# A dilated mixer taken head pair by head pair: values first, attention steps between projections

## The chip, the cores and the metric

The kernel runs on one core of one Trainium2 chip. Time is device microseconds (us) of that core. TensorE multiplies matrices into PSUM, which has eight banks of 512 columns; VectorE and ScalarE work on vectors; GpSimd and SyncE here do little but issue DMA.

## What is computed

A model of two transformer blocks and a second part, on 256 tokens of width 1024. The change lies in the second block's mixer, the dilated one: three groups of 16 heads of 64, each with its own window and dilation, combined by the softmax over all three groups' scores.

```python
DIL_GROUPS = ((128, 1), (512, 4), (2048, 16))
...
proj = (h @ w_in).reshape(B, S, N_DIL_GROUPS, 3, DIL_HEADS, DIL_HEAD_DIM)
for gi, (window, dilation) in enumerate(DIL_GROUPS):
    q = rms_norm(proj[:, :, gi, 0], g_q[gi])
    k = rms_norm(proj[:, :, gi, 1], g_k[gi])
    v = proj[:, :, gi, 2]
    ...
    o, lse = dilated_group(q, k, v, pos, table, window, dilation)
...
wts = jax.nn.softmax(jnp.stack(lses, axis=0), axis=0)
o = jnp.einsum('gbsh,gbshd->bshd', wts.astype(o_all.dtype), o_all)
return o.reshape(B, S, DIL_HEADS * DIL_HEAD_DIM) @ w_o
```

Inside a group, scores are q k / 8 plus a bias looked up by the distance of the positions, with a window mask.

## The kernel before

Five programs are written out by hand, one for each engine, and they meet in semaphores. Each program walks the same list of **units** (`PLAN`): a unit is 128 x 1024 weights, loaded by SyncE into one of four raw buffers, split by ScalarE into a high half (`wh`, line 851) and by VectorE into the rest (`wl`, line 1359), with three split buffers. On ScalarE and VectorE, entering unit u (`unit`, `ahead`) makes the halves of unit u+2, and ScalarE waits there for TensorE to have finished unit u-1. TensorE then runs 24 matmuls a unit: high by high, high by rest, rest by high (lines 346 to 348).

In the mixer the units are, for each of three groups, 16 of queries and keys (`dil_qk`, each 128 outputs of one of six kinds z) and 8 of values (`dil_v`). Two units of one kind fill a bank. Then the head norm: ScalarE squares the bank, TensorE sums the squares over each head (`head_sums`), ScalarE makes mean and root and squares the root, VectorE refines it and scales the bank into `qk` (`head_norm`). Beside the first units runs `bias(0)`: TensorE multiplies comparisons (`step`, made by VectorE) with the bias table, VectorE adds the mask into `B`. Every few units VectorE multiplies a row of modulation weights (`araw`, `tick`), whose DMA GpSimd issues.

After all 72 units come 32 attention steps, 16 heads for the first 128 tokens and 16 for the second, with `bias(1)` alone between them, because `B` holds one table. A step i does the scores of i (`s1`), turns the weights of i-2 (`s2`) and multiplies those of i-3 with the values (`s3`). VectorE adds the bias and finds the maximum, ScalarE takes the exponential, VectorE normalizes, ScalarE copies the turned weights to a buffer of three. Then `residual` runs 8 output units (`dil_w_o`), each giving 128 outputs; after each pair VectorE updates the residual `xT`, and ScalarE squares it for the next norm.

PSUM banks are taken from a queue in order of release (`take`, `give`): TensorE waits for the reader of the bank at its head. What decides the order around the change is the text of these loops.

## Time and profile before

| | us |
|---|---|
| median of 3 runs | 2232.82 (2232.3 to 2234.47) |
| the profiled execution | 2235.26 |
| its span | 2233.2 |
| TensorE busy in the span | 2035.8 |
| VectorE busy | 1459.5 |
| ScalarE busy | 1089.2 |
| issue to landing of a load of `dil_qk` | 3.7 |
| issue to landing of a load of `dil_v` | 4.2 |

All times in the rows are us from the span's start. TensorE's matmuls overlap, so the pitch from one start to the next tells more than a duration. The granted clock is a share of 2.4 GHz. In the stretches the busy times come in the order PE (TensorE), PEld (its weight loads), DVE (VectorE), ACT (ScalarE), POOL (GpSimd), each with its count of instructions. In a timeline a row "x2" is two operations from the first's start to the last's end; brackets give the idle time ahead and what ended it.

### The profile page before, as it was taken

To read this page: it belongs to the slowest core of one execution; us is meant where nothing else is said; L and a number is where in the kernel's file an instruction comes from. 1 tells how busy PE (TensorE), PEld (TensorE's weight loads), DVE (VectorE), ACT (ScalarE), POOL (GpSimd) and SP (SyncE) were. 2 spreads that over 40 slices of the span, in tenths; PEclk is the share of its full clock that TensorE was granted. 3 is DMA by queue.
4 is the path that set the end of the run, shared out by engine and by line. 5 is a ranking of instruction groups with operands and counts; after the bars stand their busy time and mean duration, and the time that the engine had idled before them with its cause. 6 is when DMAs were issued, how large, how long until landed. Compare 5 with 4: busy or idle time off the path is not lost.

```text
span 2233.2 us, 34387 instructions
## 1 busy us (share of the span) xinstructions
PE 2035.8 (91%) x14140; PEld 1873.7 (84%) x14140; DVE 1459.5 (65%) x2577; ACT 1089.2 (49%) x1676; POOL 172.2 (8%) x243
## 2 busy tenths in 40 slices
PE   2768999899999998998978889999999879999998
PEld 2646999789998978998858889999999767888886
DVE  6696885666766556744755444888886696555554
ACT  3544553335664145543654444444444695444444
POOL 3020000000000000000000000000000393000000
PEclk7879999889999699999899999999999999999999
DMA  6534687425554014665413434555555303555553
GB/s 261 195 118 147 209 282 250 157 95 201 205 170 147 10 52 157 189 189 165 175 66 123 146 122 158 171 189 184 185 188 183 112 1 113 189 188 189 188 189 122
DMA packets 97083, 356.20 MB, mean 160 GB/s; under 512 B 10704, under 2 KB 10832, under 8 KB 96544
## 3 DMA queue, kind: packets, MB, share of 16 engines
q1 hardware_dynamic: 83824, 305.04, 40.7%
q0 software_dynamic: 12672, 48.08, 6.9%
q8 instruction: 111, 1.82, 0.3%
q10 hardware_dynamic: 432, 0.90, 0.1%
q14 instruction: 44, 0.36, 0.1%
HBM read 352.93 MB, written 1.05 MB: 159 GB/s over the span
## 4 chain that ended last, share of the span: by engine, by line
PE 79%; DVE 15%; ACT 4%; DMA 1%; issue 1%; SPq 0%; POOL 0%; DVEq 0%; ACTq 0%
PE psum L346 23%; PE psum L347 22%; PE psum L348 22%; PE psum L339 10%; DVE C L1331 2%; PE psum L353 1%; DVE wl L1359 1%; DVE araw L1342 1%; DVE one L1331 1%; ACT work L839 1%; DVE one L1336 1%; DVE work L1339 1%; DMA first<-in_ada_w 1%; DVE first L1342 0%; ACT sqh L839 0%
## 5 line engine op out<-in xcount | busy, mean ns | idle before, releaser
L1359 DVE TENSOR_TENSOR wl<-raw,wh 128x1024 fp32r<-128x1024 f32 (+1 forms) x564 | 686.5, 1222 | 466.2 <-ACT wh L851 465.2
L851 ACT ACTIVATE wh<-raw 128x1024 fp32r<-128x1024 f32 (+1 forms) x564 | 592.7, 1052 | 466.0 <-PE psum L348 466.0
L346 PE MATMUL psum<-peer_hh,wh 128*128 128x256 f32 x1152 | 325.4, 282 | 4.1 <-DVE peer_hl L1331 4.0
L347 PE MATMUL psum<-peer_hl,wh 128*128 128x256 f32 x1152 | 324.5, 282 | 0.0
L348 PE MATMUL psum<-peer_hh,wl 128*128 128x256 f32 x1152 | 324.4, 282 | 0.0
L346 PEld LDWEIGHTS psum<-peer_hh,wh 128*128 128x128 f32 x1152 | 217.8, 189 | 5.4 <-DVE peer_hl L1331 4.4
L347 PEld LDWEIGHTS psum<-peer_hl,wh 128*128 128x128 f32 x1152 | 218.1, 189 | 0.0
L348 PEld LDWEIGHTS psum<-peer_hh,wl 128*128 128x128 f32 x1152 | 218.0, 189 | 0.0
L346 PE MATMUL psum<-wh,csh 128*128 128x512 f32 x512 | 202.3, 395 | 0.0
L347 PE MATMUL psum<-wl,csh 128*128 128x512 f32 x512 | 202.2, 395 | 0.0
L348 PE MATMUL psum<-wh,csl 128*128 128x512 f32 x512 | 202.2, 395 | 0.0
L346 PE MATMUL psum<-mlp_hh,wh 128*128 128x256 f32 x512 | 148.1, 289 | 8.3 <-DVE mlp_hl L1339 8.3
L347 PE MATMUL psum<-mlp_hl,wh 128*128 128x256 f32 x512 | 145.9, 285 | 0.0
L348 PE MATMUL psum<-mlp_hh,wl 128*128 128x256 f32 x512 | 145.8, 285 | 0.0
L347 PE MATMUL psum<-h1l,wh 128*128 128x256 f32 x512 | 144.1, 281 | 0.0
L346 PE MATMUL psum<-h1h,wh 128*128 128x256 f32 x512 | 144.1, 281 | 0.0
L348 PE MATMUL psum<-h1h,wl 128*128 128x256 f32 x512 | 144.1, 281 | 0.0
L346 PE MATMUL psum<-dil_hh,wh 128*128 128x256 f32 x448 | 137.9, 308 | 6.0 <-DVE dil_hl L1339 4.1
L347 PE MATMUL psum<-dil_hl,wh 128*128 128x256 f32 x448 | 130.2, 291 | 0.0
L348 PE MATMUL psum<-dil_hh,wl 128*128 128x256 f32 x448 | 130.2, 291 | 0.0
L346 PEld LDWEIGHTS psum<-wh,csh 128*128 128x128 f32 x512 | 96.0, 187 | 23.5
L348 PEld LDWEIGHTS psum<-wh,csl 128*128 128x128 f32 x512 | 96.0, 187 | 23.5
(412 smaller groups left out, 4603.4 us busy)
## 6 DMA issues: line engine op xcount, KB each, us to landing
raw<-in_mlp_w SPq DMA_DIRECT2D x128, 512.0 KB, 4.1
raw<-in_eu SPq DMA_DIRECT2D x128, 512.0 KB, 3.3
raw<-in_ev SPq DMA_DIRECT2D x128, 512.0 KB, 3.2
araw<-in_ada_w POOLq DMA_DIRECT2D x80, 512.0 KB, 4.2
raw<-in_dil_qk SPq DMA_DIRECT2D x48, 512.0 KB, 3.7
raw<-in_dil_v SPq DMA_DIRECT2D x24, 512.0 KB, 4.2
first<-in_ada_w SPq DMA_DIRECT2D x8, 1024.0 KB, 18.2
raw<-in_w_in SPq DMA_DIRECT2D x16, 512.0 KB, 3.3
```

What stands on the lines that cost most here:

```text
L339: i = e.matmul(o, l, r, start=start, stop=stop, skip_group_check=loose)
L346: e.matmul(o, l[0], r[0], start=start, stop=False, skip_group_check=loose)
L347: e.matmul(o, l[0], r[1], start=False, stop=False, skip_group_check=loose)
L348: i = e.matmul(o, l[1], r[0], start=False, stop=stop, skip_group_check=loose)
L353: t = e.transpose(o, i, ident)
L839: e.activation(o, i, f, **kw).then_inc(S.act, 1)
L851: e.activation(b.wh[v % NSPLIT][:, 0:cols], b.raw[v % NRAW][:, 0:cols], ACT.Copy).then_inc(S.hi, 1)
L1331: return op(e.tensor_tensor(o, x, y, f), mark)
L1336: return op(e.tensor_scalar(o, x, s1, s2, f0, f1), mark)
L1339: return op(e.scalar_tensor_tensor(out=o, in0=x, scalar=s, in1=y, op0=f0, op1=f1), mark)
L1342: return op(e.tensor_tensor_reduce(out=o, in0=x, in1=y, scale=1.0, scalar=init, op0=f0, op1=f1, accum_out=acc), mark)
L1359: e.tensor_tensor(b.wl[v % NSPLIT][:, 0:cols], b.raw[v % NRAW][:, 0:cols], b.wh[v % NSPLIT][:, 0:cols].bitcast(F32), ALU.subtract).then_in ...
```

## The change

The mixer is taken head pair by head pair. `dil_order` writes out one order that all programs follow. First 18 of the 24 value units (heads 0 to 11), with both bias tables beside them; `B` now holds both. Then for each pair c its six query and key units (z = 0 to 5: query and key of three groups, so a bank holds the query and key of one group), the head norms of pair c, and between them the steps of pair c-1. The roots of a pair's three groups are taken together, one pair later, behind unit z=1 of the next pair; their squares and the scales follow behind z=2 and z=3. The last six value units stand behind the last pair, and then the output units, which are now rows of the output matrix: each takes one head pair's output and adds to all 1024 outputs, in four banks that are read at the very end. The turned weights have one buffer in place of three. The modulation products come once in four value units and once in two query and key units.

```diff
+def dil_order():
+
+    values = [("dil_v", 8 * g + x, x // 2) for g in range(3) for x in range(8)]
+    out = [e for e in values if e[2] < 3] + [("biased", 0, 0)]
+    summed = []
+
+    def after_unit():
+        if summed:
+            c, g = summed.pop(0)
+            out.append(("sum", c, g))
+            if g:
+                out.append(("mean", c, g))
+
+    for c in range(8):
+        steps = {4: 4 * c - 4, 5: 4 * c - 3, 0: 4 * c - 6, 1: 4 * c - 5}
+        for z in range(6):
+            out.append(("dil_qk", 8 * z + c, z))
+            after_unit()
+            if z == 3:
+                out.append(("mean", c, 0))
+            if z % 2:
+                out.append(("square", c, z // 2))
+                summed.append((c, z // 2))
+            if steps.get(z, -1) >= 0:
+                out.append(("step", steps[z], 0))
+            if c and z == 1:
+                out.append(("root", c - 1, 0))
+            if c and z == 2:
+                out += [("root square", c - 1, 0), ("scale", c - 1, 0), ("scale", c - 1, 1)]
+            if c and z == 3:
+                out.append(("scale", c - 1, 2))
+    late = [e for e in values if e[2] == 3]
+    out.append(late[0])
+    after_unit()
+    out += [late[1], ("step", 26, 0), ("root", 7, 0), late[2], ("root square", 7, 0), ("scale", 7, 0), late[3],
+            ("scale", 7, 1), ("scale", 7, 2), late[4], late[5]]
+    for e in ((27,), 0, (28,), 1, (29,), 2, (30,), 3, 4, (31,), 5, (32,), (33,), (34,), 6, 7):
+        out.append(("step", e[0], 0) if isinstance(e, tuple) else ("dil_w_o", e, 0))
+    return out
+
+
+DIL_ORDER = dil_order()
...
-    for g in range(3):
-        add("dil_qk", 16, first=16 * g)
-        add("dil_v", 8, first=8 * g)
-    add("dil_w_o", 8)
+    for kind, i, j in DIL_ORDER:
+        if kind in ("dil_v", "dil_qk", "dil_w_o"):
+            add(kind, 1, first=i)
...
+        def head_sums(c, g):
+
+            ps = take("headsum", c, g)
+            pe.wait_ge(S.act, at["head square", c, g])
+            mm(ps, blk, m.hsq[:, (3 * c + g) % 4, :], True, True, mark=("headsum", c, g))
+            give("headsum", c, g, sem=S.act, key=("headsum", "ms", c, g))
...
+            pe.wait_ge(S.dve, at["dqk", "out", c, 2])
...
+        def step(i):
...
             if i < 32:
                 s1(i)
+            if 0 <= i - 3 < 32:
+                s3(i - 3)
             if 0 <= i - 2 < 32:
                 s2(i - 2)
-            if 0 <= i - 3 < 32:
-                s3(i - 3)
-        residual("dil_o", "dil_w_o", m.hh, lambda k: (S.dve, ("dil", "out", 3)), m.work)
+
+        def rows(i):
+            if i == 0:
+                for c2 in range(4):
+                    take("dil_o", c2)
+            j = weights("dil_w_o", i)
+            pe.wait_ge(S.dve, at["dil", "out", i])
+            for c in range(8):
+                o = b.psum[:, at["bank", "dil_o", c // 2], (c % 2) * 256:(c % 2) * 256 + 256]
+                w, x = wsp(j, c * 128, 128), m.o[:, i]
+                first, last = i == 0 and c % 2 == 0, i == 7 and c % 2 == 1
+                mm(o, w[0], x[:, 0, :], first, False, loose=True)
+                mm(o, w[0], x[:, 1, :], False, False, loose=True)
+                if c == 7:
+                    e.matmul(o, w[1], x[:, 0, :], start=False, stop=last, skip_group_check=True).then_inc(S.unit, 1)
+                else:
+                    mm(o, w[1], x[:, 0, :], False, last, loose=True,
...
+        for kind, i, z in DIL_ORDER:
+            if kind == "dil_v":
+                values(i, z)
+                next(side, None)
+            elif kind == "biased":
+                for _ in side:
+                    pass
+            elif kind == "dil_qk":
+                c = i % 8
+                if z % 2 == 0:
+                    take("dqk", c, z // 2)
+                ps = b.psum[:, at["bank", "dqk", c, z // 2], (z % 2) * 256:(z % 2) * 256 + 256]
+                j = weights("dil_qk", i)
+                for k in range(8):
+                    mm3(ps, wsp(j, k * 128, 128), sp(m.hh, k), k == 0, k == 7, unit=k == 7)
+            elif kind == "sum":
+                head_sums(i, z)
+            elif kind == "scale":
+                give("dqk", i, z, sem=S.dve, key=("dqk", "out", i, z))
+            elif kind == "step":
+                step(i)
+            elif kind == "dil_w_o":
+                rows(i)
+        for c2 in range(4):
+            give("dil_o", c2, sem=S.dve, key=("dil_o", "out", c2))
+            square_sums("dil_o", c2, m.work)
...
+                if i >= 3:
+                    ac.wait_ge(S.pe, at["dil", "pv", i - 3])
                 ac.wait_ge(S.pe, at["dil", "turned", i - 2])
-                act(wk[3 + (i - 2) % 3], bank("dt", i - 2), ACT.Copy, mark=("dil", "probT", i - 2))
-            if 0 <= i - 3 and (i - 3) % 8 == 7:
-                u = i - 3
-                t, c0 = u // 16, (u % 16) // 8 * 4
-                ac.wait_ge(S.pe, at["dil", "pv", u])
-                act(m.hh[0].rearrange("p (c t) -> p c t", c=8)[:, c0:c0 + 4, t * 128:t * 128 + 128],
-                    bank("do", u // 8).rearrange("p (c t) -> p c t", c=4), ACT.Copy, mark=("dil", "o hi", u // 8))
-        residual("dil_o", "dil_w_o", m.work)
+                act(wk[3], bank("dt", i - 2), ACT.Copy, mark=("dil", "probT", i - 2))
...
+        for kind, i, z in DIL_ORDER:
+            if kind == "dil_v":
+                u = unit("dil_v", i)
+                if i % 2:
+                    g = i // 8
+                    ac.wait_ge(S.unit, u + 1)
+                    ac.wait_ge(S.dve, at["n2", "lo", 7])
+                    act(m.vt[:, 2 * z:2 * z + 2, g, :, :],
+                        bank("dv", g, z).rearrange("p (t c n) -> p c t n", t=2, c=2), ACT.Copy, mark=("dv", "out", g, z))
+            elif kind == "biased":
+                ac.wait_ge(S.dve, at["bias", "out", 1, 7])
+                ac.wait_ge(S.dve, at["bias", "own out", 1, 7, 1])
+            elif kind in ("dil_qk", "dil_w_o"):
+                u = unit(kind, i)
+            elif kind == "square":
+                ac.wait_ge(S.unit, u + 1)
+                past = 3 * i + z - 4
+                if past >= 0:
+                    ac.wait_ge(S.dve, at["dqk", "out", past // 3, past % 3])
+                act(m.hsq[:, (past + 4) % 4, :], bank("dqk", i, z), ACT.Square, mark=("head square", i, z))
+            elif kind == "mean":
+                if i:
+                    ac.wait_ge(S.dve, at["dqk", "out", i - 1, z])
+                ac.wait_ge(S.pe, at["headsum", i, z])
+                act(m.hw[:, 0, z, :], bank("headsum", i, z), ACT.Identity, scale=1.0 / 64, bias=eps,
+                    mark=("headsum", "ms", i, z))
+            elif kind == "root":
+                ac.wait_ge(S.act, n[0])
+                for g in range(3):
+                    act(m.hw[:, 1, g, :], m.hw[:, 0, g, :], ACT.Abs_reciprocal_sqrt, mark=("root", i, g))
+            elif kind == "root square":
+                for g in range(3):
+                    ac.wait_ge(S.act, at["root", i, g])
+                    act(m.hsq[:, (3 * i + g) % 4, :], m.hw[:, 1, g, :], ACT.Square, mark=("head rs0", i, g))
+            elif kind == "step":
+                step(i)
+        for c2 in range(4):
+            square("dil_o", c2, m.work, ("dil_o", "out", c2))
...
+        def head_norm(c, g):
+            sq, ms, y = m.hsq[:, (3 * c + g) % 4, :], m.hw[:, 0, g, :], m.hw[:, 1, g, :]
+            ve.wait_ge(S.act, at["head rs0", c, g])
+            stt(sq, ms, -0.5, sq, ALU.mult, ALU.mult)
+            own()
+            stt(sq, sq, 1.5, y, ALU.add, ALU.mult)
+            own()
+            if c >= 2:
+                ve.wait_ge(S.pe, at["dil", "scores", 4 * (c - 2) + 3])
+            ps = bank("dqk", c, g)
+            for x, gain in enumerate(("dil_g_q", "dil_g_k")):
+                z = slice(256 * x, 256 * x + 256)
+                stt(m.qk[:, c % 2, 2 * g + x, :], ps[:, z], vc(b, gain, g), sq[:, z], ALU.mult, ALU.mult,
+                    mark=("dqk", "out", c, g))
...
+        for kind, i, z in DIL_ORDER:
+            if kind in ("dil_v", "dil_qk", "dil_w_o"):
+                u = unit(kind, i)
+                if kind == "dil_v":
+                    next(side, None)
+                    tick(4)
+                elif kind == "dil_qk":
+                    tick(2)
+            elif kind == "biased":
+                for _ in side:
+                    pass
+            elif kind == "scale":
+                head_norm(i, z)
+            elif kind == "step":
+                step(i)
         mod_until(80)
         own()
-        residual("dil_o", "dil_w_o", lambda c: b.mod[:, 64 + c:65 + c])
+        for c in range(8):
+            if c < 6:
+                ve.wait_ge(S.pe, at["dil_o", "done", c // 2])
+            else:
+                ve.wait_ge(S.unit, u + 1)
+            xs = b.xT[:, c * 256:c * 256 + 256]
+            stt(xs, bank("dil_o", c // 2)[:, (c % 2) * 256:(c % 2) * 256 + 256], b.mod[:, 64 + c:65 + c], xs, ALU.mult,
+                ALU.add, mark=("dil_o", "out", c // 2))
...
-        tick(72, 4)
-        tick(16, 3)
-        po.wait_ge(S.dve, at["bias", "out", 0, 7])
-        e.dma_start(m.maskc, d["mask"][:, 512:1024]).then_inc(S.mask, 16)
-        tick(19, 3)
+        tick(24, 4)
+        tick(48, 2)
+        mod_until(80)
```

**ScalarE, around a head norm in the projections.** `work<-psum` is the square, `work<-psum,con` the mean. Before:

```order
L839 ACTIVATE work<-psum 128x512 [waits s_unit]
L851 ACTIVATE wh<-raw 128x1024 [waits s_raw0]
L839 ACTIVATE work<-psum,con 128x512 [waits s_pe]
L839 ACTIVATE work<-work 128x512 [waits s_act] x2
L851 ACTIVATE wh<-raw 128x1024 [waits s_unit,s_raw1]
L839 ACTIVATE work<-psum 128x512 [waits s_unit]
```

After, behind unit z=1 of a pair, from a step's copy of turned weights on:

```order
L904 ACTIVATE work<-psum 128x512 [waits s_pe]
L904 ACT_TABLE_LOAD
L904 ACTIVATE head_work<-head_work 128x512 [waits s_act]
L904 ACTIVATE head_work<-head_work 128x512 x2
L916 ACTIVATE wh<-raw 128x1024 [waits s_raw0]
L904 ACTIVATE head_squares<-head_work 128x512 [waits s_act] x3
L916 ACTIVATE wh<-raw 128x1024 [waits s_unit,s_raw1]
L904 ACTIVATE head_work<-psum,con 128x512 [waits s_pe,s_dve]
L904 ACTIVATE head_squares<-psum 128x512 [waits s_unit]
L916 ACTIVATE wh<-raw 128x1024 [waits s_raw2]
```

The root and its square stood together behind each mean. Now three roots stand behind a step, with a table load ahead and a weight split between roots and squares, and the next mean and square stand behind them.

**VectorE, the scales in the projections.** Before:

```order
L1359 TENSOR_TENSOR wl<-raw,wh 128x1024 [waits s_hi] x2
L1339 SCALAR_TENSOR_TENSOR work<-work 128x512 [waits s_act]
L1339 SCALAR_TENSOR_TENSOR work<-work 128x512 [waits s_dve]
L1339 SCALAR_TENSOR_TENSOR qk<-psum,vec,work 128x512 [waits s_dve]
L1359 TENSOR_TENSOR wl<-raw,wh 128x1024 [waits s_hi] x2
L1339 SCALAR_TENSOR_TENSOR work<-work 128x512 [waits s_act]
```

After, behind unit z=2 of a pair (`ISA` on `araw` is the modulation product):

```order
L1423 TENSOR_TENSOR wl<-raw,wh 128x1024 [waits s_hi]
L1406 ISA araw,mod<-araw,cond 128x1024 [waits s_ada0]
L1406 ISA mod 128x1
L1403 SCALAR_TENSOR_TENSOR head_squares<-head_work,head_squares 128x512 [waits s_act]
L1403 SCALAR_TENSOR_TENSOR head_squares<-head_squares,head_work 128x512 [waits s_dve]
L1403 SCALAR_TENSOR_TENSOR qk<-psum,vec,head_squares 128x256 [waits s_dve]
L1403 SCALAR_TENSOR_TENSOR qk<-psum,vec,head_squares 128x256
L1403 SCALAR_TENSOR_TENSOR head_squares<-head_work,head_squares 128x512 [waits s_act]
L1403 SCALAR_TENSOR_TENSOR head_squares<-head_squares,head_work 128x512 [waits s_dve]
L1403 SCALAR_TENSOR_TENSOR qk<-psum,vec,head_squares 128x256 [waits s_dve]
L1403 SCALAR_TENSOR_TENSOR qk<-psum,vec,head_squares 128x256
L1423 TENSOR_TENSOR wl<-raw,wh 128x1024 [waits s_hi]
```

One scale stood between two splits. Now two stand together behind a split and a modulation product, and the third behind the next split.

**TensorE, a step.** `qk` are scores, `work,vt` weights times values, `con,work` turning. Before, in the attention:

```order
L353 MATMUL psum<-con,work 128x128 x3
L339 MATMUL psum<-work,vt 64x128 [waits s_act]
L339 MATMUL psum<-work,vt 64x128 x3
L339 MATMUL psum<-qk 128x256
L339 MATMUL psum<-qk 128x128 x2
L353 MATMUL psum<-con,work 128x128 [waits s_dve]
```

After, behind unit z=4 of a pair:

```order
L397 MATMUL psum<-dil_hh,wl 128x256
L388 MATMUL psum<-head_squares,con 128x512 [waits s_act]
L388 MATMUL psum<-qk 128x256 [waits s_dve]
L388 MATMUL psum<-qk 128x128 x2
L388 MATMUL psum<-work,vt 64x128 [waits s_act]
L388 MATMUL psum<-work,vt 64x128 x3
L402 MATMUL psum<-con,work 128x128 [waits s_dve]
L402 MATMUL psum<-con,work 128x128 x3
```

The step stood between other steps. Now it stands behind a projection unit and a head sum, and its scores wait for VectorE.

## Rows read from the trace of the kernel before

**Rows 1.** The page, TensorE's granted clock in 40 slices, in tenths:
```profile
PEclk7879999889999699999899999999999999999999
```

**Rows 2.** TensorE in order of time: start, us, operation, idle before:
```profile
429.07 0.30 PE L339 MATMUL psum<-tabsh,step 128*128 128x64 f32 x1 [1.61 <-DVE step L1339]
...
855.38 0.28 PE L348 MATMUL psum<-dil_hh,wl 128*128 128x256 f32 x1
...
862.55 0.55 PE L346 MATMUL psum<-mlp_hh,wh 128*128 128x256 f32 x1 [4.13 <-DVE mlp_hl L1339]
```

**Rows 3.** Stretches: length, then busy us of each engine, granted clock, DMA share, GB/s:
```profile
429.00:855.40 426.40, 411.37 (x2892) 377.63 (x2892) 261.26 (x447) 189.30 (x291) 12.24 (x24) 0.91 0.37 125
560.00:692.00 132.00, 129.85 (x1007) 120.99 (x1007) 87.78 (x102) 77.53 (x104) 4.23 (x8) 1.00 0.57 195
741.50:778.00 36.50, 36.48 (x167) 35.95 (x168) 17.90 (x35) 0.00 (x0) 0.00 (x0) 0.50 0.00 0
```

**Rows 4.** TensorE in order of time, a head sum and a projection unit behind it:
```profile
504.23 1.02 PE L339 MATMUL psum<-work,con 128*128 128x512 f32 x2
...
505.20 0.28 PE L347 MATMUL psum<-dil_hl,wh 128*128 128x256 f32 x1
...
510.66 0.28 PE L348 MATMUL psum<-dil_hh,wl 128*128 128x256 f32 x1
```

**Rows 5.** TensorE in order of time, products of the first bias table:
```profile
451.45 0.28 PE L339 MATMUL psum<-tabsl,step 128*128 128x64 f32 x1
...
454.83 0.28 PE L339 MATMUL psum<-tabsl,step 128*128 128x128 f32 x1
```

**Rows 6.** All engines in order of time, one attention step and the next:
```profile
712.46 1.14 PE L339 MATMUL psum<-qk 64*128 64x256 f32 x6
...
714.66 0.72 ACT L839 ACTIVATE work<-work,dst 128x512 f32<-128x512 f32 x1 [1.38 <-DVE dst L1335]
...
715.13 1.14 PE L339 MATMUL psum<-qk 64*128 64x256 f32 x6
...
715.38 0.57 ACT L839 ACTIVATE work<-psum 128x512 f32<-128x512 f32 x1
```

**Rows 7.** VectorE in order of time: residual update, modulation product, head scale and split:
```profile
408.98 3.23 DVE L1339 SCALAR_TENSOR_TENSOR xT<-psum,mod,xT 128x256 f32<-128x256 f32 x8 [0.55 <-PE psum L348]
...
573.48 1.22 DVE L1342 CUSTOM_DVE_ANT_0 araw<-araw,cond 128x1024 f32<-128x1024 f32 x1
...
577.92 1.42 DVE L1339 SCALAR_TENSOR_TENSOR work<-work 128x512 f32<-128x512 f32 x2 [0.94 <-ACT work L839]
...
580.04 2.35 DVE L1359 TENSOR_TENSOR wl<-raw,wh 128x1024 fp32r<-128x1024 f32 x2
```

**Rows 8.** Groups of the mixer by form: busy us, mean ns, idle before and its releaser:
```profile
L851 ACT ACTIVATE wh<-raw 128x1024 fp32r<-128x1024 f32 x80 | 83.8, 1049 | 18.9 <-PE psum L348 18.9
...
L1339 DVE SCALAR_TENSOR_TENSOR step<-pF,con 128x512 fp32r<-128x512 f32 x32 | 23.6, 749 | 24.7 <-PE psum L339 24.2
...
L1331 DVE TENSOR_TENSOR B<-psum,maskc 128x256 f32<-128x256 f32 x32 | 11.3, 412 | 0.4 <-PE psum L339 0.4
L1331 DVE TENSOR_TENSOR B<-psum,maskc 128x512 f32<-128x512 f32 x16 | 10.9, 683 | 2.4 <-PE psum L339 2.4
```

**Rows 9.** TensorE in order of time, its longest wait beside the first bias table:
```profile
464.94 0.48 PE L339 MATMUL psum<-tabsh,step 128*128 128x128 f32 x1 [3.48 <-DVE B L1331]
```

**Rows 10.** Stretches as in rows 3, behind that wait and in a later mixer:
```profile
468.00:471.00 3.00, 3.00 (x16) 3.00 (x16) 2.76 (x6) 0.00 (x0) 0.00 (x0) 0.50 0.38 115
...
1146.00:1148.00 2.00, 0.00 (x0) 0.00 (x0) 1.65 (x9) 1.82 (x7) 0.00 (x0) 1.00 0.00 0
```

**Rows 11.** ScalarE in order of time: two chained roots, table load, exponential:
```profile
576.59 1.30 ACT L839 ACTIVATE work<-work 128x512 f32<-128x512 f32 x2
...
695.05 1.28 ACT L839 ACT_TABLE_LOAD   x1
...
696.43 0.72 ACT L839 ACTIVATE work<-work,dst 128x512 f32<-128x512 f32 x1
```

245 lines of the change are left out of this document (80 added, 165 removed).

## The prediction

> **What bounds the kernel now.** I read the page first: its strip, in slices of 56 us, shows TensorE's granted clock at 0.6 to 0.8 in a few slices [rows 1]; the slice at 0.6 lies in the mixer. The change touches only the dilated mixer, so the rest was read as a table of stretches inside it. From the first bias product at 429.07 to the last output product at 855.38 [rows 2], 426.3 us, TensorE is busy 411.4 us and its mean clock is 0.91 [rows 3]: about 9% of 426, some 38 us, is what the lower of the two clock levels (1.2 for 2.4 GHz) costs, and some 15 us is idle. The largest piece of the 38 is the second bias table, which stands alone between the two halves of the attention: 36.5 us at clock 0.50 [rows 3], 18 us lost. Where projections run alone, 560 to 692, the clock is 1.00 and 130 of 132 us are busy [rows 3]. So here the mixer is bound by TensorE's issue, and by nothing else but the low clock and a few waits.
>
> **What TensorE has to do after the change.** The same products, in another order. Each by its pitch at full clock:
> - a projection, value or output unit, 24 matmuls: from 505.20 to 510.66 there are 46 steps, 0.1187 us each, so 2.85 us [rows 4];
> - a head sum: 504.23 to 505.20 less one pitch, 0.85 us [rows 4]; 24 of them before and after;
> - a bias product: 451.45 to 454.83 is 30 steps, 0.113 us; 384 of them are 43 us [rows 5];
> - an attention step (scores, weights times values, turning): 712.46 to 715.13, 2.67 us [rows 6]; 32 of them are 85.4 us. They already run back to back, so putting them between projections hides nothing of TensorE's own time.
>
> The output units are the same 24 matmuls in another nesting; I take the same pitch. The new evacuations and copies are of shapes near those shown, and none is TensorE's.
>
> **Part 1, values and both bias tables first.** Today the first bias product is at 429.07 [rows 2]. Its compare stands behind one modulation product on VectorE (1.14 us, [rows 7]), and the change puts the compare ahead: 427.9. From there to the end of the tables: 16 units, 45.6 us, and 43 us of bias, at full clock 516.5. In this stretch TensorE holds at most one value bank beside the bias banks, and every bank it takes was to be emptied one unit earlier; VectorE needs 5.2 us for an iteration with the wide products (a split 1.17 [rows 7], an evacuation of 0.68 and four of 0.41, two compares of 0.75 [rows 8], a quarter of a modulation product) against 2.85 + 3.6 = 6.45 on TensorE. I take no stall in it. I add one low-clock episode after the start, as now, and one at the end, where two wide bias pieces (7.2 us) stand in a row, and a short wait for the last compare: 3 + 4 + 0.8. Price of an episode: TensorE stood still for 3.48 us up to 464.94 [rows 9] and then ran at 0.50 up to 471 [rows 10], 6 us, so 3 us lost. That gives 524.3. The gain of the change is here: the 18 us of the second table.
>
> **Part 2, the head pairs.** Six units, three head sums and four steps are 17.1 + 2.55 + 10.7 = 30.3 us a pair. What decides is one chain. The steps of pair c-1 begin behind unit z=4 of pair c, and their scores wait for the third scale of pair c-1. Call T the end of unit z=1.
>
> TensorE reaches unit z=4's end at T + 2.67 (step) + 2.85 + 0.85 + 2.85 + 2.85 = T+12.1, and would start the step, after one head sum, at T+12.9.
>
> The chain: scores begin at T; ScalarE's exponential starts 2.20 later (712.46 to 714.66), the copy behind it at 715.38 ends at 715.95 [rows 6]: T+3.5. Then a table load, since the exponential's table is in: 1.28 [rows 11], T+4.8. Three roots: two dependent ones took 1.30 [rows 11]; in a row without waits 0.53 each (between 0.53 and 0.65), T+6.4. The high half of the next weights, 1.05 [rows 8]: T+7.45. VectorE has its split 1.17 behind that, T+8.65, then in five of the seven pairs a modulation product 1.14, T+9.8. Then two scales, each two 512-column operations (1.42, [rows 7]) and two of 256 columns, in the present form 577.92 to 580.04, 2.12, and a split second half adds 0.15: 2.27 each, T+14.35. Then, by its program, the split for unit z=5, 1.17, and only then the third scale: T+17.8.
>
> So the step waits from about T+12.9 to T+17.8, 5.0 us in all. It falls in two parts: the head sum ahead of the step waits 1.5 us, because its square stands behind the mean that waits for the first scale (T+12.1), and the scores wait 3.5. Without the modulation product it is 3.85 in all. Pair 1 has no step and no table load ahead of its roots, but the steps behind z=0 and z=1 are missing on TensorE too: 3.5. Sum over pairs 1 to 7: 3.5 + 2 x 3.85 + 4 x 5.0 = 31.2 us. Bounds: 0 (if the chain is shorter by what it exceeds) and 45 (2 us more a pair for handoffs that no row has). I take 31, since each link but the 256-column one has a row.
>
> Weights arrive: the high halves that this stretch needs are issued after splits that lie over 9 us back, and a load lands in about 4 us, so the DMA queue is not late; GpSimd's queue issues as many modulation rows as before.
>
> **Part 3, the clock.** Each of these stalls is an idle of 3.5 us, after 1.5 us of idle and 0.85 of work. The one of 3.48 us ahead of 464.94 was followed by 6 us at 0.50 [rows 9, 10]. One of 2 us, at 1146 to 1148, left the clock at 1.00 [rows 10]. I take the first, the nearer in length: 3 us lost a pair, 21 us. Bounds 0 and 30.
>
> **Part 4, the end.** Behind the last pair the split for the first output unit stands behind three scales: about 2.3 us. The last three steps have no unit between them, and the single buffer of turned weights makes TensorE wait twice for a copy, 1.5 us. Now the output rows collect in four banks to the very end, so eight residual updates (8 took 3.23 us, [rows 7]) stand there, six of which may start within the last unit; and the exponential's table is still in, so the root's load of 1.28 falls into this tail. At present it takes 862.55 - 855.38 = 7.2 us to the next product [rows 2]; I work out 9.3.
>
> **The sum.** 524.3 + 62 units (176.7) + 20.4 + 85.4 = 806.8; + 31.2 + 21 + 2.3 + 1.5 = 862.8; + 5, the share of idle that no wait above explains (2 of 132 us in the calm stretch [rows 3], over 390 us, nearly 6) = 868; next product at 877 against 862.55. That is **14 us later**. The profiled execution took 2235.3 us (span 2233.2), so 2249; on the median of the three runs, 2232.8, it is 2247. I give 2246. About 0.2% is what a measurement can tell from no change.
>
> **A rule weighed.** In 694.4 to 696.5 a table load lasts 1.28 us and the exponential starts 0.10 us after its end [rows 11]; the trace has nothing of a drain between. The Trainium skill, "ScalarE: Activation LUTs", section "What ACT_TABLE_LOAD costs", gives about 1.28 us for the load and as much again for a drain, 2.66 in all. By it each of the seven chains would be 1.38 us longer, and the result 10 us slower still. The row speaks against it.
>
> **The rivals.**
> 1. *The stalls are there, but the clock holds.* For it: the idle of 2 us that cost no clock [rows 10]. Against it: the one of 3.5 us. Then 14 - 21 = -7 us, 2226, **faster**; it decides if the idle pieces stay near 2 us. Chance 18%.
> 2. *No stall.* If ScalarE's roots came 5 us sooner relative to TensorE. Nothing in the rows makes it so; -7 - 31 = -38 us, 2195. Chance 8%.
> 3. *The clock stays low through much of each pair.* For it: 36.5 us on end at 0.50 with TensorE busy throughout [rows 3]. Against it: that was narrow bias work. 15 us low instead of 6, 4.5 x 7 = +31, 2278. It decides if 5 us of idle in 35 keep the level down. Chance 11%.
> 4. *The bias pieces pull the clock down even between value units.* Then the 89 us of part 1 run largely at half: +40 us or so, and the change does not do what it says. Against it: 451 to 455 ran such products at full pitch [rows 5]. Chance 4%.
> 5. *A drain behind each table load*, as in the rule above: a gap of 1.4 us between load and root, +10 us, 2256. Chance 2%.
>
> **How the numbers follow.** My forecast, stalls with a lost clock, has 57%; its own range is 2233 to 2258. Faster by over 0.2% (below 2228): most of rival 1 (12), rival 2 (8), and 3 of the forecast, 23%. Within 0.2%: 6 of rival 1 and 10 of the forecast, 16%. Slower: 61%. The range 2217 to 2266 leaves out rival 2 and most of rivals 3 and 4, about 2 in 10.
>
> **What would show it.** In the stretches of the new trace: the second table's 36.5 us at 0.50 gone; in each pair from the second on a wait of TensorE for VectorE's write of the queries and keys, about 3.5 us, ahead of one step in four, and a shorter one for ScalarE's square; the clock at 0.5 for about 6 us behind it; a load of 1.28 us between a copy and the three roots; the pair's period near 38 us. If the period is 30 to 32 us, part 2 is wrong; if it is 35 at clock 1.00, part 3 is.

## The result, and the profile after

| | before | changed |
|---|---|---|
| median, same chip | 2231.96 us | 2238.73 us |
| lowest to highest | 2228.91 to 2237.31 | 2234.5 to 2241.7 |
| ratio, 95% interval | | 1.0029, 1.0022 to 1.0037 |
| profiled execution (span) | 2235.26 (2233.2) | 2236.3 (2234.5) |

The change makes the kernel 0.3% slower, 6.5 us by the ratio. The forecast was 14 us slower. Direction and mechanism hold; the size is less than half of it.

In the page's strip of the granted clock every slice behind the eighth is at 9, where [rows 1] has one at 6 and two at 8:

```profile
PEclk7879999899999999999999999999999999999999
```

TensorE in order of time gives the marks of the mixer: its first product, first and last bias product, last output product and the first product of the next stage (start, us, operation, idle ahead of it and its releaser). They answer to [rows 2]:

```profile
415.63 0.55 PE L395 MATMUL psum<-wh,dil_hh 128*128 128x256 f32 x1 [4.13 <-DVE dil_hl L1403]
424.75 0.30 PE L388 MATMUL psum<-tabsh,step 128*128 128x64 f32 x1 [0.80 <-DVE step L1403]
519.26 0.42 PE L388 MATMUL psum<-tabsl,step 128*128 128x128 f32 x1
...
856.18 0.28 PE L726 MATMUL psum<-dil_o,wl 128*128 128x256 f32 x1
...
866.74 0.55 PE L395 MATMUL psum<-mlp_hh,wh 128*128 128x256 f32 x1 [4.13 <-DVE mlp_hl L1403]
```

The first product came 3 us earlier than in the trace of before (418.67), for reasons that lie ahead of the mixer, so I count from it: the next stage begins 866.74 - 415.63 = 451.1 us later, against 862.55 - 418.67 = 443.9 before. That is +7.2 us, which agrees with the measured +6.5. The two traces as wholes differ by only 1.3 us (spans 2234.5 and 2233.2), since the part behind the mixer is 2.9 us shorter as well. Neither of these 3 us can be put down to the change: in the twelve traces of this document the mixer begins at 415.6 to 420.3 us, and 1367 to 1377 us lie behind it, with the same program in both parts.

The same stretch cut at the first scores behind unit z=4 of each pair (length, busy us of PE, PEld, DVE, ACT, POOL, then granted clock, DMA share, GB/s):

```profile
424.75:521.00 96.25, 96.25 (x775) 96.25 (x776) 68.21 (x106) 21.08 (x25) 2.65 (x5) 0.92 0.37 126
521.00:560.25 39.25, 35.98 (x269) 33.23 (x267) 24.44 (x33) 21.02 (x28) 2.65 (x5) 0.98 0.61 199
560.25:593.59 33.34, 29.89 (x191) 26.28 (x191) 19.99 (x40) 19.46 (x30) 0.53 (x1) 0.90 0.34 110
...
630.36:667.99 37.63, 33.04 (x223) 28.77 (x223) 23.17 (x46) 20.81 (x33) 1.58 (x3) 0.91 0.40 128
...
780.12:856.50 76.38, 72.83 (x538) 66.39 (x538) 41.29 (x79) 35.94 (x57) 1.06 (x2) 0.96 0.38 119
```

The values and both bias tables now run in one piece, with TensorE busy in all 96.25 us, at 0.92; the 36.5 us at 0.50 of [rows 3] are gone. In exchange the pair shown (630.36 to 667.99) takes 37.63 us where its work is 30.3, with 4.6 us of idle and a clock of 0.91. The waits of one pair, TensorE in order of time:

```profile
663.59 1.10 PE L388 MATMUL psum<-head_squares,con 128*128 128x512 f32 x2 [1.29 <-ACT head_squares L904]
...
667.99 2.05 PE L388 MATMUL psum<-qk 64*128 64x256 f32 x6 [3.30 <-DVE qk L1403]
...
675.89 1.14 PE L388 MATMUL psum<-qk 64*128 64x256 f32 x6
```

The second wait, of 3.27 to 3.31 us, stands in all seven pairs that have one before them (pairs 1 to 7); the first, of 1.28 or 1.29, in pairs 3, 4, 5 and 7, those with a modulation product in the chain. From 667.99 to 675.89 a unit and a step take 7.90 us; the next time, in 682.27 to 687.79, they take 5.52. The level fell during the idle and stayed down some 5 us behind it:

```profile
666.00:669.00 3.00, 1.01 (x3) 0.86 (x4) 2.93 (x6) 0.78 (x1) 0.00 (x0) 0.55 0.51 175
669.00:672.00 3.00, 3.00 (x14) 2.44 (x13) 2.53 (x7) 0.81 (x2) 0.53 (x1) 0.50 0.59 186
672.00:675.00 3.00, 3.00 (x22) 3.00 (x23) 0.35 (x1) 1.55 (x2) 0.00 (x0) 0.82 0.49 164
```

And the chain behind the wait. ScalarE, then VectorE, from the step behind unit z=1 (its scores start at 650.16, the T of the forecast) to the scores at 667.99:

```profile
652.36 0.72 ACT L904 ACTIVATE work<-work,dst 128x512 f32<-128x512 f32 x1 [1.50 <-DVE dst L1399]
...
653.68 1.28 ACT L904 ACT_TABLE_LOAD   x1
654.97 1.67 ACT L904 ACTIVATE head_work<-head_work 128x512 f32<-128x512 f32 x3
656.55 1.05 ACT L916 ACTIVATE wh<-raw 128x1024 fp32r<-128x1024 f32 x1
```

```profile
657.63 1.23 DVE L1423 TENSOR_TENSOR wl<-raw,wh 128x1024 fp32r<-128x1024 f32 x1 [4.70 <-ACT wh L916]
658.77 1.22 DVE L1406 CUSTOM_DVE_ANT_0 araw<-araw,cond 128x1024 f32<-128x1024 f32 x1
...
659.91 0.69 DVE L1403 SCALAR_TENSOR_TENSOR head_squares<-head_work,head_squares 128x512 f32<-128x512 f32 x1
...
661.36 0.88 DVE L1403 SCALAR_TENSOR_TENSOR qk<-psum,vec,head_squares 128x256 f32<-128x256 f32 x2
...
663.60 0.88 DVE L1403 SCALAR_TENSOR_TENSOR qk<-psum,vec,head_squares 128x256 f32<-128x256 f32 x2
664.39 1.22 DVE L1423 TENSOR_TENSOR wl<-raw,wh 128x1024 fp32r<-128x1024 f32 x1
...
666.97 0.88 DVE L1403 SCALAR_TENSOR_TENSOR qk<-psum,vec,head_squares 128x256 f32<-128x256 f32 x2
```

From 657.63 to 667.8 VectorE does not stop once: split, modulation product, two scales, split, third scale. The scores start 0.14 us behind the end of the last row (666.97 + 0.88).

### The profile page after: what moved, and what is told of

Its sections match the earlier page's. It is cut to its first block, busy times and chain, and to the rows that moved or that the text cites. A ratio compares the mean times of both kernels' runs of the same rounds, so it can differ in the third digit from the quotient of the medians.

```text
span 2234.5 us, 34482 instructions
## 1 busy us (share of the span) xinstructions
PE 2020.7 (90%) x14140; PEld 1857.4 (83%) x14140; DVE 1463.3 (65%) x2605; ACT 1103.9 (49%) x1694; POOL 171.6 (8%) x242
## 4 chain that ended last, share of the span: by engine, by line
PE 77%; DVE 16%; ACT 5%; DMA 1%; issue 1%; SPq 0%; POOL 0%; DVEq 0%; ACTq 0%
PE psum L395 22%; PE psum L397 22%; PE psum L396 22%; PE psum L388 10%; DVE wl L1423 2%; DVE C L1395 2%; PE psum L402 1%; DVE one L1395 1%; DVE head_squares L1403 1%; DVE araw L1406 1%; DVE one L1400 1%; DVE qk L1403 1%; DMA first<-in_ada_w 1%; ACT L904 1%; ACT wh L916 1%
## 5 line engine op out<-in xcount | busy, mean ns | idle before, releaser
L395 PE MATMUL psum<-dil_hh,wh 128*128 128x256 f32 x384 | 117.9, 307 | 0.0
L904 ACT ACTIVATE C<-psum 128x512 f32<-128x512 f32 x84 | 50.4, 599 | 132.4 <-PE psum L397 128.9
L396 PEld LDWEIGHTS psum<-wl,csh 128*128 128x128 f32 x512 | 96.1, 188 | 23.2
```

Of the source, the lines that this page charges most:

```text
L395: e.matmul(o, l[0], r[0], start=start, stop=False, skip_group_check=loose)
L396: e.matmul(o, l[0], r[1], start=False, stop=False, skip_group_check=loose)
L904: e.activation(o, i, f, **kw).then_inc(S.act, 1)
```

## Experiments

Each kernel is the changed one with the edit shown. Each ran on one chip together with the kernel before, but not all of them on the same chip, so I compare ratios to that kernel: the changed one stands at 1.0029, so a ratio r lies (1.0029 - r) x 2232 us below it. An interval of a ratio is 2 to 4 us wide to each side. The last column is one trace of each: from the mixer's first product to the first product of the next stage, 451.1 us in the changed kernel and 443.9 in the one before.

| kernel | median us | ratio to before, 95% interval | against the changed kernel | mixer in its trace, us |
|---|---|---|---|---|
| roots one unit sooner | 2211.9 | 0.9892, 0.9873 to 0.991 | -31 us | 423.3 |
| modulation products at odd units | 2238.76 | 1.0023, 1.0011 to 1.0035 | -1, within the intervals | 451.6 |
| TensorE kept busy in the waits | 2220.01 | 0.9936, 0.9919 to 0.9952 | -21 | 434.5 |
| no table load | 2230.68 | 0.999, 0.9977 to 1.0004 | -9 | 439.7 |
| third scale ahead of the split | 2229.67 | 0.9981, 0.9972 to 0.999 | -11 | 441.4 |
| second table alone | 2254.59 | 1.0099, 1.0085 to 1.0113 | +16 | 462.8 |
| roots, squares and scales sooner | 2211.81 | 0.9902, 0.9887 to 0.9917 | -28 | 422.7 |
| the same, and the table early | 2207.06 | 0.9883, 0.9868 to 0.9898 | -33 | 420.2 |
| the table early, alone | 2238.46 | 1.0022, 1.0013 to 1.0031 | -2, within the intervals | 450.0 |
| **squares behind the step** | **2197.5** | **0.9841, 0.9825 to 0.9857** | **-42** | **405.3** |

### 1. Do the narrow products lose their clock for standing alone?

```diff
-                next(side, None)
+                if 6 * (i // 8) + i % 8 < 10:
+                    next(side, None)
```

The edit stands in the value branch of TensorE's and VectorE's programs; the second table then runs where the branch "biased" drains what is left.

> The changed kernel, with the first bias table beside the first ten value units as it is, but the second table's eight iterations behind the eighteenth value unit in a row, with no unit between them (both tables still ahead of the head pairs). Theory (the gain of the change lies in the second table running beside units): alone it ran 36.5 us at clock 0.50 in the kernel before, so about 18 us are lost again, 2239 + 18 = 2257. Rival: the second table was slow for its place behind the attention and not for being alone, and the total stays at 2239; or the low level lasts only for its first half, 2248.

Measured: 1.0099, 16 us slower than the changed kernel. The second table's products alone, stretches as above:

```profile
500.00:530.00 30.00, 29.82 (x147) 29.71 (x147) 16.00 (x29) 0.00 (x0) 0.00 (x0) 0.53 0.01 2
```

They run on to 534.7 at this pace: again some 35 us at half clock, now ahead of the attention and not within it. So it was being alone, not the place, that made them slow. In the traces the mixer is 11.7 us longer, not 16, but 5 us of the difference lie elsewhere: with the same instructions, the changed kernel's trace ran at 0.79 in 424 to 448 us, and this one at 1.00 in the same part. Without that it is 17 us, so running the second table beside the value units is worth 16 to 17 us. This is the gain of the change, and it is there.

### 2. Is it one VectorE chain that ends the wait?

```diff
-                out += [("root square", c - 1, 0), ("scale", c - 1, 0), ("scale", c - 1, 1)]
-            if c and z == 3:
-                out.append(("scale", c - 1, 2))
+                out += [("root square", c - 1, 0), ("scale", c - 1, 0), ("scale", c - 1, 1), ("scale", c - 1, 2)]
```

> The third scale stands directly behind the second, ahead of VectorE's split for unit z=5 (1.17 us) and not behind it. Theory (one VectorE chain ends the stall): the wait ahead of the scores falls from 3.3 to about 2.1 us in pairs 3, 4, 5, 7 and from 3.3 to 2.1 in the others, 7 x 1.17 = 8 us, and the clock still falls behind it, since 1.92 us of idle did that in the run with the roots one unit sooner: about 2230.5. Rival A (the split for z=5 is what unit z=5 then waits for): the same 1.17 us is lost one unit later, 2239. Rival B (a wait near 2 us costs no clock here, as the row at 1146 to 1148 of the kernel before has it): 8 + 17 us, 2214.

Measured: 0.9981, 11 us faster. Taking the 1.17 us split out of the chain shortened the wait in each of the seven pairs by 1.1 us:

```profile
661.35 1.10 PE L386 MATMUL psum<-head_squares,con 128*128 128x512 f32 x2 [1.29 <-ACT head_squares L902]
664.60 1.59 PE L386 MATMUL psum<-qk 64*128 64x256 f32 x6 [2.16 <-DVE qk L1401]
```

The 2.16 us still cost the clock: 0.57 or 0.79 in the 8 us behind each (rival B falls). The split was needed nowhere sooner (rival A falls).

The modulation product was moved within the same chain:

```diff
-                elif kind == "dil_qk":
-                    tick(2)
+                elif kind == "dil_qk" and z % 2:
+                    tick()
```

> The changed kernel with VectorE's modulation products behind the odd units of a pair (z=1, 3, 5) in place of the even ones. Theory (the product behind z=2 is a link of the chain; it is the whole of the first stall): behind z=2 the chain loses 1.14 us, but the product behind z=3 now stands ahead of the third scale, so the first stall of 1.29 us falls to about 0.15 and the second of 3.30 grows by 1.14 to 4.4 in four pairs; total within 2 us of the changed kernel. Rival (what stands ahead of the first scale costs more than what stands ahead of the third, since the first also starts the low clock): 5 us or more faster than the changed kernel.

Measured: 1.0023, no difference that can be told. In TensorE's waits the first lost 0.95 us and the second gained 1.15, so that their sum is about what it was (4.79 against 4.59 us):

```profile
665.65 1.10 PE L388 MATMUL psum<-head_squares,con 128*128 128x512 f32 x2 [0.34 <-ACT head_squares L904]
671.19 2.04 PE L388 MATMUL psum<-qk 64*128 64x256 f32 x6 [4.45 <-DVE qk L1403]
```

At odd units the product stands behind the first two scales and ahead of the third: the chain to the third scale is as long as it was, only the head sum's part of it is shorter.

### 3. Does a drain come on top of the table load?

```diff
-                    act(m.hw[:, 1, g, :], m.hw[:, 0, g, :], ACT.Abs_reciprocal_sqrt, mark=("root", i, g))
+                    act(m.hw[:, 1, g, :], m.hw[:, 0, g, :], ACT.Identity, mark=("root", i, g))
```

This leaves out the true root, and with it the two table loads of each pair.

> The changed kernel with the head norm's root replaced by a plain copy (it leaves out the true root, so its output differs): ScalarE then has no table loads in the pairs. Theory (one table load of 1.28 us is a link of each of six chains, and nothing more than 1.28): the stalls shrink by 1.28 us a pair in pairs 2 to 7, 7.7 us, plus up to 3 us if the clock falls later; 8 to 11 us faster than the changed kernel. Rival (a drain goes with the load, 2.66 us in all): 2.66 a pair, 16 us or more faster. Rival (the load is hidden): no change.

Measured: 0.999, 9 us faster. ScalarE in order of time, copy and roots: the roots start 0.03 us behind the copy's end (652.33 + 0.58 = 652.91), and the gap in which the changed kernel had its load is closed.

```profile
652.33 0.58 ACT L904 ACTIVATE work<-psum 128x512 f32<-128x512 f32 x1
652.94 1.67 ACT L904 ACTIVATE head_work<-head_work 128x512 f32<-128x512 f32 x3
```

The first wait is gone (1.29 us) in pairs 3, 4, 5 and 7, and the second is 2.40 in place of 3.30 us in pairs 2 and 6. A load costs 1.28 us and nothing more (rival 5 falls). In the changed kernel it starts at 653.68 and the root at 654.97, 0.01 us behind its end. The Trainium skill, "ScalarE: Activation LUTs", section "What ACT_TABLE_LOAD costs", puts a drain beside the load, 2.66 us in all; these rows disagree, as the row did that the forecast took.

### 4. What does the clock cost, apart from the idle?

TensorE gets four products that nobody reads, ahead of each of these waits, so that it stands still no longer but waits as long:

```diff
+            if u % 4 == 0 and u < 28:
+                for _ in range(4):
+                    mm(ps, ident, m.B[:, 0, 0, :], True, True)
             pe.wait_ge(S.dve, at["dqk", "out", c, 2])
```

> The changed kernel with four extra matmuls of 512 columns on TensorE (0.85 us each, written to the scores' bank and overwritten) ahead of the wait of the first scores of each of seven pairs: work in place of most of the 3.3 us of idle. The output is not changed by it. Theory (the idle lets the clock fall, 2.4 us lost a pair): the second stall is work now, the clock stays at full level, the period falls by about 2.3 us, 14 to 17 us less than the changed kernel, ratio to before about 0.996. Rival (the low stretches come from the kind of work in the step, not from the idle): the low stretches stay, and the kernel is as the changed one or up to 2 us slower.

Measured: 0.9936, 21 us faster by the ratio, 19 by the medians, 16.6 in the mixer's trace. TensorE in order of time, then the stretch of a pair:

```profile
660.25 1.10 PE L388 MATMUL psum<-head_squares,con 128*128 128x512 f32 x2 [1.29 <-ACT head_squares L907]
661.19 3.60 PE L388 MATMUL psum<-B,con 128*128 128x512 f32 x8
664.71 1.14 PE L388 MATMUL psum<-qk 64*128 64x256 f32 x6
```

```profile
620.00:656.00 36.00, 34.71 (x238) 28.96 (x238) 23.78 (x47) 21.39 (x35) 1.59 (x3) 1.00 0.41 132
```

The wait is as long (from the head sum's start to the scores' 4.46 us, against 4.40 in the changed kernel), and the clock is 1.00. So the low level behind the seven waits costs some 17 us by itself, and filling the idle is enough to remove it: with the same work around them the pairs run at full clock (rival 3 falls).

### 5. Roots sooner: how much of it is the order?

Roots behind unit z=0 ahead of the step there, their squares behind z=1, the scales behind z=1, 2 and 3:

```diff
+            if c and z == 0:
+                out.append(("root", c - 1, 0))
+            if c and z == 1:
+                out.append(("root square", c - 1, 0))
             if steps.get(z, -1) >= 0:
                 out.append(("step", steps[z], 0))
             if c and z == 1:
-                out.append(("root", c - 1, 0))
+                out.append(("scale", c - 1, 0))
             if c and z == 2:
-                out += [("root square", c - 1, 0), ("scale", c - 1, 0), ("scale", c - 1, 1)]
+                out.append(("scale", c - 1, 1))
             if c and z == 3:
                 out.append(("scale", c - 1, 2))
```

> The changed kernel with the three roots of a pair moved one unit earlier, ahead of the step behind z=0, their squares ahead of the step behind z=1, and the scales one behind each of z=1, 2 and 3. Theory (the chain from a step on ScalarE through roots and scales to the next pair's scores sets TensorE's two stalls a pair, and these let the clock fall): the chain ends some 5 us earlier, the stalls of 1.29 and 3.30 us go or fall below 1 us, the low stretches behind them go, the pair's period falls from 37.6 to about 31 us, and the kernel gains 28 + 16 = about 44 us on the changed one, 37 on the one before (ratio to before about 0.983). Rival (the order matters little, since VectorE is nearly full and another wait takes the place): within 10 us of the changed kernel, ratio 1.000 or above.

Measured: 0.9892, 31 us faster than the changed kernel, not 44. The wait is 1.92 us in most pairs, not 0. The clock falls behind it, but not behind the one of 0.78 us in the pair without a modulation product (8 us from the end of each):

```profile
655.35:663.35 8.00, 8.00 (x48) 7.29 (x48) 4.76 (x9) 2.84 (x5) 0.53 (x1) 0.79 0.54 164
721.91:729.91 8.00, 8.00 (x60) 7.16 (x61) 5.90 (x14) 3.13 (x7) 0.53 (x1) 1.00 0.55 167
```

The whole chain moved by one unit, but VectorE's part of it spread: it now has a scale, a split, a modulation product, a scale, a split, a scale.

Then all of it a further unit sooner, roots and squares both ahead of the step behind z=0:

```diff
+            if c and z == 0:
+                out += [("root", c - 1, 0), ("root square", c - 1, 0)]
             if steps.get(z, -1) >= 0:
                 out.append(("step", steps[z], 0))
+            if c and z < 3:
+                out.append(("scale", c - 1, z))
```

(The lines for roots and scales behind it are gone.)

> The roots and their squares both behind unit z=0, ahead of the step there, and the scales behind units 0, 1 and 2, each one unit sooner than in the run with only the roots early. Theory: that run had 10.8 us of waits for the queries and keys left and some 12 us of low clock behind five of them (2.5 us each); with the chain a further unit sooner no scores wait, the clock stays up, 2212 - 10.8 - 12 = about 2189, and the stretch from pair 1 to pair 7 shows a granted clock of 1.00. Rival: the exponential of the step behind z=0 now stands behind two table loads and six operations of 0.55 us, about 1.7 us later than it was, and its weights are late by that much: the wait moves to ScalarE's copy, 7 x 1.7 = 12 us, about 2201 or, with the clock falling behind each, 2212 as before.

Measured: 0.9902, no gain over the run before. The rival held: no scores wait any more, but two table loads, three roots and three squares now stand ahead of ScalarE's exponential, and TensorE waits for its copy instead. ScalarE, then TensorE:

```profile
667.93 1.28 ACT L902 ACT_TABLE_LOAD   x1
669.23 1.67 ACT L902 ACTIVATE head_work<-head_work 128x512 f32<-128x512 f32 x3
670.81 1.66 ACT L902 ACTIVATE head_squares<-head_work 128x512 f32<-128x512 f32 x3
672.48 1.28 ACT L902 ACT_TABLE_LOAD   x1
673.77 0.72 ACT L902 ACTIVATE work<-work,dst 128x512 f32<-128x512 f32 x1
```

```profile
675.21 1.06 PE L386 MATMUL psum<-work,vt 128*64 128x128 f32 x8 [1.44 <-ACT work L902]
```

The squares need not stand there, since no table changes for them (no load stands between roots and squares above). Put behind the step, and with the tail's table load moved (next experiment):

```diff
+            if c and z == 0:
+                out.append(("root", c - 1, 0))
             if steps.get(z, -1) >= 0:
                 out.append(("step", steps[z], 0))
+            if c and z == 0:
+                out.append(("root square", c - 1, 0))
+            if c and z < 3:
+                out.append(("scale", c - 1, z))
```

> The three roots ahead of the step behind unit z=0 (as in the run with only the roots early), their squares behind that step, the scales behind units 0, 1 and 2, and the root's table loaded behind the last step. Theory: the waits of 1.44 us for ScalarE's copy in the runs with the squares ahead of the step came from the exponential standing 1.7 us later; with the squares behind it they go, and the third scale is as early as there, so that no scores wait: 2207 less 7 x 1.44 = 10 us and less 6 us of low clock behind the longest, about 2192. Rival: the squares (1.7 us) now stand ahead of ScalarE's high half for the next unit, VectorE's split is late by as much, and units z=2 wait for their weights instead, 0.7 to 1.7 us a pair: 2200 to 2207.

Measured: 0.9841, 42 us faster than the changed kernel and 35 us faster than the one before: the best version here. The theory held but for 5 us, and the rival in its weakest form: from 611 us on one unit of each pair waits 0.77 us for its weights. In the pairs the waits for ScalarE's copy are down to a single one of 0.90 us. The trace shows 45.8 us less in the mixer than the changed kernel's, but 5.2 of them lie in the tables' part, whose instructions are the same in both: it happened to lose 3.4 us to the low clock here and 8.6 there.

The stretch from the end of the tables to the output rows:

```profile
521.00:774.00 253.00, 245.36 (x1798) 217.15 (x1797) 174.15 (x328) 160.86 (x252) 10.09 (x19) 1.00 0.46 148
```

The clock is 1.00 throughout. A pair takes 31.4 us where the one shown above took 37.63.

### 6. The tail

```diff
             elif kind == "step":
                 step(i)
+                if i == 34:
+                    act(b.col[:, 60:61], eps, ACT.Abs_reciprocal_sqrt)
```

> As the run with roots and scales early, and one root of a single column on ScalarE behind the last attention step, so that the root's table is loaded while TensorE still runs output units; the squares at the end of the mixer then find it in. Theory: the load of 1.28 us stands in the chain of the tail (10.56 us from the last output product to the next product in the changed kernel, 7.17 in the one before), so this gives 1.3 us: the tail 9.3 and about 1.3 us less than the run beside it. Rival: ScalarE's load is hidden behind VectorE's eight updates (3.23 us), nothing, the tail stays at 10.5.

> The changed kernel with one edit: a root of a single column on ScalarE behind the last attention step, so that the root's table is in before the squares at the end of the mixer. Theory: the tail of 10.56 us becomes about 9.4 (with the roots and scales early it went from 10.57 to 9.39), 1.2 us in all, 2237.5. Rival: the run with both edits was 4.7 us faster than the one without this one because the shorter standstill leaves the clock up in the next stage: then 4 to 5 us here too, 2234.

Measured: 4.7 us with the early scales (2211.81 to 2207.06), but alone no difference that can be told (1.0022, where 1.2 us would be 0.0005). The tail itself shows it in both, 9.39 and 9.41 us from the last output product to the next product, where it was 10.57 and 10.56. So 1.2 us it is, and the load was not hidden behind the eight updates (the rival for the first run falls). The other 3.5 of the 4.7 are not shown to come from the edit: the intervals of those two ratios overlap, and their traces differ by 2.5 us in the mixer, 1.2 in the tail and 1.3 in the pairs. There the clock did not fall behind the waits of 1.44 us at 708 and 740 us, as it had at 708 and 741 without the edit, though the order of instructions is the same. The rival for the second run (4 to 5 us from the next stage) falls.

## Why the prediction was half right

Its own terms against the trace, from the first bias product to the last output product:

| term | forecast, us | measured, us |
|---|---|---|
| work: 78 units, sums, steps, bias | 371.1 | 371.1 (pitches as before: 5.52 for a unit and a step) |
| waits in the pairs, counted as the forecast did | 31.2 | 30.7 |
| low clock behind them | 21 | 18.5 |
| low clock in the tables' part | 7 | 8.5 |
| wait for the last compare | 0.8 | 0 |
| splits of the output rows; last steps | 2.3; 1.5 | 2.0; 1.5 |
| remainder | 5 | -0.9, by difference |
| sum | 440 | 431.4 |
| from there to the next product | 9.3 | 10.56 |

The clock terms are (1 - granted clock) x length, summed over the 8 us behind each wait and over the low pieces at 424 to 448 and 516 to 523. The forecast measured a wait from where the pitches would let the scores start (T + 12.9, where T is the end of unit z=1) to where they start; so does the table. TensorE's idle alone is 28.2 us, since the products ahead of a wait last longer than their pitch (a head sum 1.10 us against 0.85).

**Part 1 held.** The tables end 94.5 us behind the first bias product against 96.4, with TensorE never idle; the second table's 36.5 us at 0.50 are gone, and putting it alone again cost 16 us (forecast 18). Rival 4 falls.

**Part 2, the chain, held to a tenth of a microsecond.** T + 17.8 was worked out for the third scale; it ended at 667.85, T + 17.7. The links between stand likewise: load done T + 4.8 (the roots start at 4.81), high half 7.45 (7.44), modulation product 9.8 (the first scale starts at 9.75), second scale 14.35 (the split starts at 14.23). The scores began at T + 17.83 (667.99), so by the forecast's own count the two waits were 4.9 us where 5.0 was taken, in pairs 3, 4, 5 and 7 alike; in pairs 2 and 6 they were 3.76 where 3.85 was taken, and in pair 1 3.5 where 3.5 was. In all 0.5 us over seven pairs. The pairs were told apart rightly: two waits in pairs 3, 4, 5 and 7, one in 1, 2 and 6. Rival 2 falls.

**Part 3 held in kind.** Every wait of 3.3 us took the clock down. The price was 1.7 to 3.4 us a pair, 2.5 to 2.8 in those with both waits, against 3. Rivals 1 and 3 fall.

**The step that failed is the last one of the sum: "+ 5, the share of idle that no wait above explains".** It was set on top of terms that already named every wait, and only on the new side. The traces show nothing in its place: the other terms already come to 0.9 us more than was measured, so 5.9 of the 8.5 us overshot are this term. The clock behind the waits is the next, 2.5 us (3 a pair where 2.65 was paid on average). The waits, the last compare and the splits add 0.5, 0.8 and 0.3, and the low clock in the tables' part takes 1.5 off again. Without the 5 us the forecast would have been 9 us slower.

Why 5 us matter so much here: beyond its 371.1 us of work the stretch cost 55 us before (426.3) and 60 after (431.4). One table's 18 us went, as did the other waits and episodes of before, and 47 us of idle and low clock (28.2 and 18.5) came in the pairs. The result is the small difference of two large sums. From the stretch +5.1 us, from its start relative to the mixer's first product -1.3 (9.12 against 10.40), from the tail +3.4 (10.56 against 7.17): +7.2.

**Part 4 failed the other way, by 1.3 us.** The forecast had six of the eight residual updates begin within the last output unit. VectorE in order of time shows why they did not: a split of later weights stands ahead of them, and the first starts behind it at 855.95, with the last output product at 856.18.

```profile
854.80 1.23 DVE L1423 TENSOR_TENSOR wl<-raw,wh 128x1024 fp32r<-128x1024 f32 x1 [1.61 <-ACT wh L916]
855.95 3.22 DVE L1403 SCALAR_TENSOR_TENSOR xT<-psum,mod,xT 128x256 f32<-128x256 f32 x8
```

All eight lie in the tail, 3.2 us, where the kernel before has two behind its last unit. No run moves that split, so this part is read from the order and not tested. The 1.28 us of the table load were foreseen.

One price in the prediction does not fit its own chain: for the drain it counts seven chains, 10 us, but says itself that pair 1 has no table load ahead of its roots. Six chains of 1.38 us are 8 us. The rival fell, so nothing hangs on it.

## What to carry to other kernels

Work put between other work is free only if what it waits for is early enough by the consumer's order: write the chain down with its start and its end against the unit that uses it, and move the link whose place is free (here three squares of 0.55 us, which may stand ahead of or behind an exponential, decided some 9 us: ratios 0.9883 and 0.9841). A wait of TensorE in each round can cost its length and then two thirds of it again in clock (28.2 and 18.5 us here). Shortening it from 3.3 to 2.2 us left 17.0 of the 18.5; with the roots one unit sooner five waits of 1.8 to 1.9 us still cost 1.7 us each; and the versions whose waits stayed at 1.35 us or less had none of it. And where a gain and a loss nearly cancel, forecast the difference, with any allowance on both sides or on neither.

## What the runs showed of the chip

**How long TensorE stood still, and whether its clock fell.** Taken over the head pairs and output rows of the changed kernel and its ten variants, the 8 us behind the end of each wait: behind waits of 0.6 to 1.35 us the mean clock was 1.00, unless a longer wait followed within them; behind all of 1.8 to 2.2 us (0.57 to 0.79) and all of 3.3 us and more (0.57 to 0.79) it had fallen. Between them the length does not decide. Waits of 1.44 us went both ways within one run:

```profile
675.21:683.21 8.00, 8.00 (x62) 7.34 (x62) 7.63 (x16) 4.78 (x9) 0.00 (x0) 1.00 0.18 66
707.94:715.94 8.00, 8.00 (x49) 7.19 (x50) 7.63 (x16) 4.78 (x9) 0.00 (x0) 0.80 0.20 66
```

And in the run without table loads both waits of 2.40 us, in pairs 2 and 6, cost nothing, while one of 2.46 us in the run with roots, squares and scales early did (0.82). Here is the first of them, TensorE alone:

```profile
592.00:595.30 3.30, 0.90 (x3) 1.00 0.39 118
595.30:598.00 2.70, 2.70 (x20) 1.00 0.34 106
```

So what else the chip goes by besides the length of one wait stays open, and with it why some episodes cost 1.7 us and others 3.4. The 2 us of idle at clock 1.00 in [rows 10] was one such case, and no guide for seven.

**The clock can fall without idle.** In the changed kernel TensorE was busy throughout 444 to 448 us, with bias products and a value unit, at 0.57:

```profile
444.00:448.00 4.00, 4.00 (x23) 4.00 (x23) 3.48 (x7) 0.00 (x0) 0.00 (x0) 0.57 0.11 34
448.00:516.00 68.00, 68.00 (x592) 68.00 (x590) 48.77 (x72) 17.26 (x20) 2.12 (x4) 1.00 0.40 138
```

The instructions of this part are the same in all eleven versions, up to the tenth value unit, and yet the traces differ. In 28.4 to 32.4 us behind the mixer's first product the clock was 0.57 in five of them, the changed kernel's included. In three it fell some 4 to 8 us sooner and was back at 1.00 there, and in the other three it was at 1.00 (no table load, second table alone, squares behind the step). So the order of the instructions alone does not decide it, and what does stays open. It also says how far one trace can be trusted: in the tables' part the low clock cost 8.5 to 8.6 us in nine of the traces and 3.4 in that of the best version.
